# A decoder layer on one core: the sample rows' output projection turned round in column strips, and three neighbouring moves in the order of ScalarE and VectorE

## The reference, cut to what matters

```python
def merge_groups(o_mla, o_dsa, g_out, w_out):
    g_a, g_b = jnp.split(g_out, [MLA_HEADS * MLA_V])
    return jnp.concatenate([rms_norm(o_mla, g_a), rms_norm(o_dsa, g_b)], axis=-1) @ w_out

def decoder_layer(x, c, pos, attend, lw):
    ...
    o_mla, o_dsa = attend(mla_t, dsa_t)
    x = x + gate_m * merge_groups(o_mla, o_dsa, lw['g_out'], lw['w_out'])
    h = rms_norm(x, lw['g_norm_ffn']) * (1 + scale_f) + shift_f
    x = x + gate_f * swiglu(h, lw['w_ffn_in'], lw['w_ffn_out'])
```

## Time and profile before

| | us |
|---|---|
| median of 3 runs | 1239.51 (1238.33 to 1242.34) |
| the profiled execution | 1241.13 |
| its span, first to last instruction | 1239.3 |
| PE busy in the span | 1168.3 (94%) |
| DVE busy | 676.0 (55%) |
| ACT busy | 401.0 (32%) |

### The profile page before, as it was taken

The page is one execution under the profiler, slowest core; times in us unless marked ns, Lnnn a source line. Parts: engine busy times, 40 slices in busy tenths (PEclk is TensorE's granted clock), DMA queues, the critical chain, the costliest instruction groups (busy, mean ns, idle before and its releaser), DMA issues.

```text
span 1239.3 us, 22240 instructions
## 1 busy us (share of the span) xinstructions
PE 1168.3 (94%) x9016; PEld 1032.9 (83%) x9016; DVE 676.0 (55%) x1510; ACT 401.0 (32%) x780; POOL 92.6 (7%) x138
## 2 busy tenths in 40 slices
PE   6699999998999999999999999889999999979997
PEld 4588896455587899999999776779999999969996
DVE  1633853745889787778877433343343343294330
ACT  3322333532477655555555333310110110100001
POOL 2000002001204400000000111000000000000000
PEclk9899999997899999999999999559999999989999
DMA  9597651021102202222222566303233233233321
GB/s 321 147 273 199 198 171 52 1 68 53 50 2 77 78 1 78 78 77 78 77 102 95 193 199 238 136 1 102 85 90 96 85 97 89 58 95 92 94 70 69
DMA packets 137738, 129.09 MB, mean 104 GB/s; under 512 B 17110, under 2 KB 131171, under 8 KB 135580
## 3 DMA queue, kind: packets, MB, share of 16 engines
q1 hardware_dynamic: 133596, 86.89, 23.8%
q0 software_dynamic: 4064, 41.11, 9.1%
HBM read 124.58 MB, written 3.41 MB: 103 GB/s over the span
## 4 chain that ended last, share of the span: by engine, by line
PE 79%; DVE 10%; DMA 4%; ACT 3%; issue 2%; SPq 1%; POOL 0%; DVEq 0%; ACTq 0%; POOLq 0%
PE psV L1187 19%; PE psV L955 12%; PE psA L1187 10%; PE psA L692 7%; PE psV L1076 3%; PE psV L892 3%; PE psA L1134 2%; PE psV L916 2%; PE psA L935 2%; PE psV L648 2%; PE psV L754 2%; PE psA L1005 1%; PE psA L903 1%; DVE wide_r L2230 1%; DMA r<-cache_idx,rows_of 1%
## 5 line engine op out<-in xcount | busy, mean ns | idle before, releaser
L955 PE MATMUL psV<-r_r,wide_r 128*128 128x260 f32 x1536 | 207.5, 288 | 3.4 <-DVE msk L2020 2.9
L955 PEld LDWEIGHTS psV<-r_r,wide_r 128*128 128x128 f32 x1536 | 190.4, 189 | 5.9 <-issue 3.3
L1466 ACT ACTIVATE wring<-psV 128x512 f32<-128x512 f32 x128 | 76.3, 597 | 91.4 <-PE psV L955 69.0
L1187 PE MATMUL psV<-qiz_r,wring_r 128*128 128x260 f32 x528 | 93.9, 283 | 0.0
L2219 DVE TENSOR_TENSOR wide<-wide,psV 128x520 f32 (+1 forms) x22 | 15.3, 697 | 137.6 <-PE psV L1187 137.6
L2021 DVE TENSOR_REDUCE msk<-wring 128x8 f32<-128x512 f32 x128 | 86.5, 676 | 0.0
L692 PE MATMUL psA<-wide_r,wring_r 128*128 128x260 f32 x432 | 79.8, 289 | 6.5 <-DVE hT_r L2261 6.4
L1187 PEld LDWEIGHTS psV<-qiz_r,wring_r 128*128 128x128 f32 x528 | 76.2, 188 | 0.0
L1187 PE MATMUL psA<-qiz_r,r_r 128*128 128x260 f32 x352 | 71.6, 285 | 1.6 <-DVE hT_r L2156 1.6
L1187 PE MATMUL psA<-qiz_r,wring_r 128*128 128x260 f32 x352 | 71.4, 285 | 0.0
L1187 PE MATMUL psA<-hT_r,r_r 128*128 128x260 f32 x352 | 71.3, 284 | 0.0
(11 more groups left out here) (501 smaller groups left out, 2556.2 us busy)
## 6 DMA issues: line engine op xcount, KB each, us to landing
wring<-w_ffn_in SPq DMA_DIRECT2D x44, 512.0 KB, 3.8
wide<-w_ada SPq DMA_DIRECT2D x11, 1024.0 KB, 6.5
wring<-w_ffn_out SPq DMA_DIRECT2D x16, 704.0 KB, 4.7
tok<-w_ada SPq DMA_DIRECT2D x9, 1024.0 KB, 6.8
wring<-w_in SPq DMA_DIRECT2D x24, 256.0 KB, 3.5
wring<-w_out SPq DMA_DIRECT2D x8, 512.0 KB, 7.2
wide<-w_out SPq DMA_DIRECT2D x2, 2048.0 KB, 8.5
wring<-w_in SPq DMA_DIRECT2D x20, 128.0 KB, 2.7
```

Source lines behind the costliest of these rows:

```text
L955: mm = pe.matmul(kx[m % 2][:, hf, :], w, wtab[:, b % 2, l, 2 * k + hf, :], start=(k == 0 and w is high and l == 0), stop=(k == 1 and w is ...
L1187: mm = pe.matmul(out[:, hf, 0:HT], w[:, k, :], x[:, hf * HT:(hf + 1) * HT], start=(k0 + k == 0 and x is xh and w is high), stop=(k0 + k == ...
L1466: A(sq2[m % 2].rearrange("p (x n) -> p x n", x=2), kx[m % 2][:, :, 0:256], ACT.Square).then_inc(kx_squared, 1)
```

## The change

The samples' mixed rows are now first scaled by the RMS factors and the gain, into `mix32` [128, 8 blocks, 32 columns], whose columns 8 to 31 are zero. `sample_rows(hf)` makes `mix32` the weights and streams 512 columns of `w_out` through: eight matmuls, block k in the column strip k % 4. So each strip of 32 PSUM partitions holds a partial sum of two blocks. ACT copies the first 512 columns to SBUF, DVE the second. `sample_turn(hf)` multiplies each block of 128 columns with a selection matrix, which adds the four strips and turns the result back to features by samples. Both halves of `w_out` are now needed before the first product. The product of half 0 before the last sample is gone.

The prompt's root moves between the key copies of sample 7, behind the exponential, with a one-element Exp after it that brings the table back. The pieces 0 and 1 of the modulation move to right behind the reciprocal, and the others one or two places forward.

```diff
-            def sample_out(g, m):
-
-                for k in range(4):
-                    mm = pe.matmul(spm[:, m, g, :], wo_half[g][:, k, m * 128:(m + 1) * 128], mixT[:, 4 * g + k, SEQ:T], start=(k == 0), stop=(k == 3),
+            def sample_rows(hf):
+
+                for k in range(KD):
+                    q = 32 * (k % 4)
+                    mm = pe.matmul(tokps[hf][q:q + 32], mix32[:, k, :], wo_half[k // 4][:, k % 4, hf * 512:(hf + 1) * 512], start=(k < 4), stop=(k >= 4),
                                    skip_group_check=True)
+                mm.then_inc(od_full, 1)
+
+            def sample_turn(hf):
+
+                pe.wait_ge(mix_copied[hf], 1)
+                for m in range(4 * hf, 4 * hf + 4):
+                    mm = pe.matmul(spm[:, m, :], tokS[:, m * 128:(m + 1) * 128], sel[:, 64:72], start=True, stop=True, skip_group_check=True)
                 return mm
...
-                if b == NB - 1:
-                    pe.wait_ge(ol_taken, 2)
-                    pe.wait_ge(wo_loaded[0], 16)
-                    for m in range(KD):
-                        sample_out(0, m)
                 weigh_values(b)
...
             values_out(NB - 1)
-            pe.wait_ge(wo_loaded[1], 16)
             pe.wait_ge(mix_s, 1)
-            for m in range(KD):
-                mm = sample_out(1, m)
-                if m == 3:
-                    pe.wait_ge(mix_s, 2)
-                    pe.matmul(ssum_mix, ones, sums2.rearrange("p g b -> p (g b)"), start=True, stop=True, skip_group_check=True).then_inc(a_full, 1)
-            mm.then_inc(od_full, 1)
+            pe.matmul(ssum_mix, ones, sums2.rearrange("p g b -> p (g b)"), start=True, stop=True, skip_group_check=True).then_inc(a_full, 1)
+            for x in range(2):
+                pe.wait_ge(wo_loaded[x], 16)
+            pe.wait_ge(mix_s, 2)
+            sample_rows(0)
+            sample_rows(1)
+            sample_turn(0)
+            sample_turn(1).then_inc(od_full, 1)
...
             for b in range(NB - 1):
+                if b == 6:
+                    high_part(0)
+                    high_part(1)
                 take(NB + b)
                 if b == 5:
+                    exps(NB + b + 1)
+                    take_keys(4 * b + 8)
+                    take_keys(4 * b + 9)
                     prompt_root()
+                    take_keys(4 * b + 10)
+                    take_keys(4 * b + 11)
+                    take_strips(b + 2)
+                    A(stat[0:1, 0, 3:4], epsc[0:1], ACT.Exp)
+                    continue
...
+            high_part(2)
             A(stat[0:1, 0, 2:3], epsc[0:1], ACT.Sqrt)
-            high_part(1)
-            high_part(2)
+            high_part(3)
+            high_part(4)
             take(2 * NB - 1)
-            for k in range(3, 7):
-                high_part(k)
+            high_part(5)
+            high_part(6)
             act.wait_ge(a_full, A_MIX + 1)
...
+            act.wait_ge(od_full, 2)
+            A(tokS[:, 0:512], tokps[0], ACT.Identity).then_inc(mix_copied[0], 1)
...
                 if b == 6:
                     v.wait_ge(v_free, V_SS2 + 1)
                     link(v.reciprocal(root2, root2))
-            modulate_prompt(v, 3)
+                    modulate_prompt(v, 0)
+                    modulate_prompt(v, 1)
             modulate_prompt(v, 4)
+            modulate_prompt(v, 5)
...
+            link(v.tensor_tensor(mixraw[:, 4:8], mixraw[:, 4:8], gT[:, G_OUT + 4:G_OUT + 8].unsqueeze(2).broadcast_to([128, 4, NB]), ALU.mult))
             modulate_prompt(v, 6)
+            modulate_prompt(v, 7)
             v.wait_ge(a_free, A_MIX + 1)
             link(v.reciprocal(rms8, rms8))
-            v.wait_ge(od_full, 2)
+            v.tensor_tensor(mix32.rearrange("p (g k) b -> p g k b", g=2)[:, :, :, 0:NB], mixraw.rearrange("p (g k) b -> p g k b", g=2),
+                            rms8.unsqueeze(2).broadcast_to([128, 2, 4, NB]), ALU.mult).then_inc(mix_s, 1)
+            modulate_prompt(v, 8)
+            v.wait_ge(od_full, 3)
+            v.tensor_copy(tokS[:, 512:1024], tokps[1]).then_inc(mix_copied[1], 1)
+            v.wait_ge(od_full, 4)
...
-            link(v.tensor_tensor(weighed, spm, rms8.unsqueeze(1).broadcast_to([128, 8, 2, NB]), ALU.mult))
-            link(v.tensor_tensor(weighed[:, :, 0, :], weighed[:, :, 0, :], weighed[:, :, 1, :], ALU.add))
-            link(v.tensor_tensor(weighed[:, :, 0, :], weighed[:, :, 0, :], modT[:, 16:24, 1:9], ALU.mult))
+            link(v.tensor_tensor(weighed, spm, modT[:, 16:24, 1:9], ALU.mult))
...
-            modulate_prompt(v, 7)
             link(v.tensor_tensor(hs, xs, amod[:, 1, :, 1:9], ALU.mult))
-            modulate_prompt(v, 8)
```

More of the change, by code:

```diff
@@ L328, in build @@
         odps = psA[:, 1, 1, 128:160].rearrange("p (k b) -> p k b", k=4)
-        spm = psA[:, 1, 1, 160:288].rearrange("p (m g b) -> p m g b", m=8, g=2)
+        spm = psA[:, 1, 1, 160:224].rearrange("p (m b) -> p m b", m=8)
+        tokps = [psA[:, x, 0, :] for x in range(2)]
         ssum_mix, ssum_ffn = psA[:, 0, 1, 256:272], psA[:, 0, 1, 272:280]
@@ L353, in build @@
         sum8, root8 = qrflat[:, 96:104], qrflat[:, 104:112]
-        weighed = qrflat[:, 128:256].rearrange("p (m g b) -> p m g b", m=8, g=2)
+        weighed = qrflat[:, 128:192].rearrange("p (m b) -> p m b", m=8)
+        mix32 = latflat[:, 640:896].rearrange("p (k b) -> p k b", k=8)
+        tokS = wflat[:, 4096:5120]
         bias_rows = nc.dram_tensor("bias_rows", [8, 384], F32, kind="Internal").ap()
@@ L408, in build @@
         sq2_written, x_new, h2_scaled, h2_high, s_summed = (sem(x) for x in ("sq2_written", "x_new", "h2_scaled", "h2_high", "s_summed"))
-        wo_loaded = [sem(f"wo_loaded{x}") for x in range(2)]
+        wo_loaded, mix_copied = ([sem(f"{name}{x}") for x in range(2)] for name in ("wo_loaded", "mix_copied"))
         y_stored = [sem(f"y_stored{s}") for s in range(2)]
@@ L1566, in act_decode @@
             for b in range(NB - 1):
+                if b == 6:
+                    high_part(0)
+                    high_part(1)
                 take(NB + b)
                 if b == 5:
+                    exps(NB + b + 1)
+                    take_keys(4 * b + 8)
+                    take_keys(4 * b + 9)
                     prompt_root()
+                    take_keys(4 * b + 10)
[3 more added lines that the diff above has]
+                    continue
                 if b + 2 < NB:
                     take_keys(4 * b + 8)
-                else:
-                    high_part(0)
                 exps(NB + b + 1)
@@ L2089, in latent_values @@
                 v.tensor_reduce(sums2[:, 0, :], sq64[:, 0:4].rearrange("p k b -> p b k"), AXX, ALU.add)
-                v.tensor_tensor(mixT[:, 0:4, SEQ:T], mixraw[:, 0:4], gT[:, G_OUT:G_OUT + 4].unsqueeze(2).broadcast_to([128, 4, NB]),
-                                ALU.mult).then_inc(ol_taken, 1)
+                v.memset(mix32, 0.0)
+                link(v.tensor_tensor(mixraw[:, 0:4], mixraw[:, 0:4], gT[:, G_OUT:G_OUT + 4].unsqueeze(2).broadcast_to([128, 4, NB]), ALU.mult))
             for b in range(NB):
@@ L2099, in dve_decode @@
                 elif b == NB - 1:
-                    modulate_prompt(v, 0)
+                    modulate_prompt(v, 2)
                 shift(NB + b)
-                if b == NB - 1:
-                    modulate_prompt(v, 1)
                 row_sums(NB + b)
@@ L2111, in dve_decode @@
                 elif b == NB - 1:
-                    modulate_prompt(v, 2)
+                    modulate_prompt(v, 3)
                 normalise(NB + b)
@@ L2132, in dve_decode @@
             link(v.tensor_tensor(sq64[:, 4:8], mixraw[:, 4:8], mixraw[:, 4:8], ALU.mult))
             v.tensor_reduce(sums2[:, 1, :], sq64[:, 4:8].rearrange("p k b -> p b k"), AXX, ALU.add).then_inc(mix_s, 1)
-            modulate_prompt(v, 5)
+            link(v.tensor_tensor(mixraw[:, 4:8], mixraw[:, 4:8], gT[:, G_OUT + 4:G_OUT + 8].unsqueeze(2).broadcast_to([128, 4, NB]), ALU.mult))
             modulate_prompt(v, 6)
+            modulate_prompt(v, 7)
             v.wait_ge(a_free, A_MIX + 1)
@@ L2145, in dve_decode @@
+            link(v.tensor_tensor(xs, xs, weighed, ALU.add))
             link(v.tensor_tensor(sq64, xs, xs, ALU.mult))
             v.tensor_reduce(sum8, sq64.rearrange("p k b -> p b k"), AXX, ALU.add).then_inc(s_summed, 1)
-            modulate_prompt(v, 7)
             link(v.tensor_tensor(hs, xs, amod[:, 1, :, 1:9], ALU.mult))
-            modulate_prompt(v, 8)
             v.wait_ge(a_free, A_SS2 + 1)
```

3 lines of the change are left out of this document (removed).

## The result

| | before | after |
|---|---|---|
| median | 1240.92 us (1238.33 to 1242.38, 4 runs) | 1223.18 us (1221.72 to 1224.99, 4 runs) |
| ratio of the times | | 0.9869, 95% interval 0.9847 to 0.9891 |
| profiled execution, span | 1241.13, 1239.3 | 1224.99, 1223.2 |

By the medians the kernel is 17.7 us faster (1.4%), against 18.8 forecast and 1221 named. The ratio in the table is not the quotient of these two medians, which is 0.9857; by it the gain is 16.3 us, with an interval of 13.5 to 19.0. First the windows by stage of the kernel after: length; busy time of PE, PEld, DVE, ACT and POOL with instructions; granted clock; DMA share; GB/s.

The account below looks back on a forecast made before the run. PE was taken to bound the path through both halves of `sample_out`, 13.8 and 14.2 us at clock 0.50. The FFN starting 19.3 us earlier, less 0.5 for its clock, gave 18.8 us won: 1221 us, range 1217.5 to 1226.

Parts of the forecast that it names:

- The root among the key copies: At sample 7's key copies: one table load less ahead of the strips, which begin 2.2 us earlier, at about 780.2.
- The softmax: Last sample, between scores and last weighting: 5.0 us with two pieces inside instead of 7.2 with three.
- The pieces ahead of `mix32`: DVE's four halves of pieces 6 and 7, 0.67 us each: `mix32` at 797.9, or 796 without pieces in the way.
- The rows: New projection in four strips: 5.55 us, with 3.2 us at the lower clock; bounds 5.2 and 7.92.
- The turns: Behind the rows: DVE's copy 0.685 us, then four matmuls, 1.7 us at the lower clock or 0.9 at the full; end 805.1.
- The FFN's clock: At the FFN's start: PE idles some 2.5 us, the clock probably falls again; 0.5 us subtracted.
- The w_out transfer: Second transfer of `w_out`, ahead of the rows: there by 796.1, hidden by 1.8 us.
- A: Rival: clock stays low through rows and turns; 3.5 us later, 1224.2; chance 0.17.
- B: Rival: ACT and DVE set the pace around table loads, softmax and `mix32`; 3.3 us later, 1224.3; chance 0.15.
- C: Rival: full clock kept to the FFN, 1.6 us won in place of 0.5 lost; 1218.6; chance 0.15.
- D: Rival: the rows' strips don't run side by side, 27.5 us instead of 5.55; about 1243, slower; chance 0.02.
- E: Rival: the change doesn't do what it says, as PE's work was hidden by something ending at the same date; chance 0.02.

Follow-up runs that it names:

- strips_only: The kernel after with the new projection kept but ScalarE's and VectorE's order of the kernel before put back; 1227.75 us, ratio 0.9902.
- root_only: The kernel after with strips, root and tables kept but the modulated pieces left where they were before; 1224.73 us, ratio 0.9891.
- early_mix: The kernel after with piece 1 behind the scores, pieces 6 and 7 behind `mix32`, ACT's Sqrt load and root ahead of high parts; 1221.39 us.
- filled: The kernel after with ten extra 512-column matmuls, results unused, at five places where PE waits; 1214.89 us, ratio 0.9816.
- one_strip: The kernel after with all eight blocks of a half accumulated in the first 32-column strip instead of four; 1234.30 us, ratio 0.9958.
- narrow_fill: The kernel after with fills at the same places as filled, each as four 8-column matmuls instead of one with 512; 1222.27 us, ratio 0.9873.
- both_two: The kernel after with early_mix's edits and dense fills, two of them behind the turns, none late in the FFN; 1211.68 us, ratio 0.9786.
- rows_twice: The kernel after with the rows' products issued twice, the second overwriting the first; 1225.73 us, ratio 0.9883.
- order_only: The kernel before with its old projection, but root, tables and pieces in the new order; 1233.55 us, ratio 0.9953.
- down_fill: The kernel after with five 512-column matmuls in one PE wait late in the FFN, nothing else filled; 1221.74 us, ratio 0.9869.

## Why the prediction was right

The forecast was 18.8 us won, and 17.7 were by the medians; 1223.18 lies in the range, and faster was right. The size is a little nearer than its parts: the FFN was forecast 19.3 us earlier and came 17.68 earlier, and from keys to output 17.1 were won. The median of before had moved from the 1239.51 of the forecast to 1240.92, and this luck makes up for some of it. To set its dates beside the trace, which began 1.43 us earlier at the keys, that is added to the measured ones:

| step | forecast | measured + 1.43 |
|---|---|---|
| key strips begin | 780.2 | 780.31 |
| scores taken | 785.5 | 785.73 |
| last weighting | 790.5 | 790.63 |
| `mix32` ready for PE | 797.9 | 797.94 |
| rows | 797.9, 5.55 us | 798.08, 6.61 us |
| turns end | 805.1 | 806.58 |
| FFN's first product | 808.4 | 809.98 |

- **The root among the key copies.** It moved the strips as forecast, and 1.5 us (1.4 forecast) were given back behind them: the scores were ready at 782.78 and taken at 784.30, because DVE's second half of piece 0 waited at 783.63 for the high part, which stood behind the table load at 781.49.
- **The softmax** took 4.90 us (forecast 5.0); strips_only and root_only, with more pieces inside, took 7.24 and 5.99.
- **The pieces ahead of `mix32`** were on the path, 793.34 to 796.08, as costed; early_mix shows them as time to be had.
- **The rows** are the term that was mis-sized: 6.61 us, where "3.2 us at the lower clock" gave 5.55. The form's price was right, even a little high at the full clock (3.64 measured in filled against 3.96). The clock rose later. The windows of the kernel after:

```profile
802.00:802.50 0.50, 0.50 (x4) 0.00 (x0) 0.00 (x0) 0.00 (x0) 0.00 (x0) 0.50 0.00 0
802.50:803.00 0.50, 0.50 (x8) 0.00 (x0) 0.00 (x0) 0.00 (x0) 0.00 (x0) 0.83 0.00 0
803.00:803.50 0.50, 0.50 (x7) 0.31 (x3) 0.18 (x1) 0.00 (x0) 0.00 (x0) 1.00 0.00 0
```

  It rose at 802.7, 6.0 us behind the start and not 2.6 to 3.2 as in the earlier trace rows. In the eight profiles that began these rows at the lower level (one_strip's among them) the rise came between 3.4 us (narrow_fill) and 6.0 behind their start, so it is a value with scatter, and the 3.2 of the prediction lies below all eight. With the turns 0.3 longer (1.90 us), the rows' start 0.2 later and the tail 0.1 to 0.2 longer (3.40) this is the 1.6 us by which the FFN came late. The turns were costed as a wait for DVE's copy and four matmuls behind it. In the trace DVE's copy is done at 804.01 and PE turns without a gap until 805.15, so all eight matmuls set the length, and not the copy.
- **The FFN's clock.** -0.5 was forecast; the stretch from the first product to DVE's first gate is 13.97 us against 13.42 before, 0.55 more. The lower level held for 4.4 us and not 3.19.
- **The w_out transfer** was hidden (issued at 785.61, landing in 8.0 us, so there at 793.6 for rows at 796.65). early_mix makes it the bound.

**The rivals.** A (clock low through the rows) came half true: rows at the lower level for 6.0 of 6.61 us, but not the turns. The Trainium skill (TensorE: Matmul & The Clock Gate, "What's actually happening") says that activity releases the throttle. The traces agree with it in part: with the fills of both_two the clock stayed at 1.00 from the keys into the FFN, but under the 8-column matmuls of the kernel before it stayed at 0.50 for 13.76 us of a PE that was busy all along. B (ACT and DVE set the pace) is refuted by the dates of the first four steps. C (clock kept to the FFN) did not happen in the kernel after and is what both_two reaches with fills. D (strips one behind the other) is refuted by the rows' 6.61 us, and one_strip shows what it would have cost: 10.0 us. At this clock that is still faster than before, so D's price was right for one matmul (16.61 us with about 5.5 of them at the lower level make 0.87 at the full clock), and wrong in holding the clock low for all of them. E is refuted by rows_twice: 3.1 us more of rows come out as 3.1 us locally.

**What stays open.** When the clock rises under the same rows (3.4 to 6.0 us behind their start in eight profiles) no run explains, nor why it fell at 778.8 in the kernel after, just ahead of the strips, and only at 783.8 in root_only. The worth of the pieces at the reciprocal, 0.1 to 0.5 us, is reckoned and not measured. How many fills are enough behind the turns rests on one profile each. Why the keys begin at dates up to 3.7 us apart, I did not look into; nothing there differs between the kernels.

## What to carry to other kernels

A product of few rows with full weight blocks pays for loading weights; with the activations as the weights, four column strips side by side and a small turn back, the one here went from 28 us to 8.5. Ahead of such a product look at what the clock will be. Filling PE's idle time with 512-column matmuls paid here where PE came last behind it (9 to 11.5 us, together with an earlier `mix32`), and not where PE only waited for another engine (0.1 us). Before adding or comparing savings in one stretch, read the granted clock of each trace: 15.3 and 7.0 us alone were 17.7 together, and some 4 us of that gap were the clock's.

## What the runs showed of the hardware

- Under an unbroken stream of 8-column matmuls with full weights the granted clock stayed at 0.50 for 13.76 us in the kernel before. It fell from 1.00 to 0.50 under such a stream twice: in narrow_fill at 787.6, 2.5 us into it, and in order_only at 783.9, only 0.7 us into it, where the 0.67 us of idle time just ahead are as good a reason.
- Sixteen matmuls of 32 weight columns by 512 in four strips took 3.64 us at the full clock; in one strip, with the clock low for the first 5.5 us, 16.61.
- The end of the kernel scatters by itself: from the output's first transposition to the last instruction it was 11.97 us in the profile before and 14.41 in the one after, with the same code. ACT's timeline before:

```profile
1228.46 1.94 ACT L1614 ACTIVATE hT<-psA 128x1024 f32<-128x1024 f32 x2 [150.46 <-PE psA L1234]
1232.31 1.02 ACT L1614 ACTIVATE hT<-psA 128x1024 f32<-128x1024 f32 x1 [1.91 <-DMA y_p<-hT]
```

  and after:

```profile
1209.91 1.94 ACT L1633 ACTIVATE hT<-psA 128x1024 f32<-128x1024 f32 x2 [150.47 <-PE psA L1241]
1216.21 1.02 ACT L1633 ACTIVATE hT<-psA 128x1024 f32<-128x1024 f32 x1 [4.36 <-DMA y_p<-hT]
```

  The wait for the store of the first tile is 4.36 us in place of 1.91. The stretch took 11.9 to 12.0 us in nine of the fourteen profiles and 13.4 to 14.4 in five; down_fill, which differs from the kernel after only far ahead of it, has 12.0. One profile's total is therefore a poor measure for a local change of 1 or 2 us; the length between two dates around it is a better one.
